# One gate pair fewer multiplied plainly: block products from pair 1, another order of the sums of h, other banks

## The reference, cut to what matters

```
h      = rms_norm(x, g) * (1 + scale) + shift
ga, gb = the last 2 x 1024 columns of h @ w_in
y_m    = (h_m * silu(za)) @ w_out_mlstm
y_a    = (o_a * silu(zb)) @ w_out_attn
merged = sigmoid(ga) * y_m + sigmoid(gb) * y_a
out    = rms_norm(x + gate * (merged @ w_out), g_final)
```

## Time and profile before

| what | us |
|---|---|
| median of 3 runs (lowest, highest) | 1432.43 (1432.05, 1433.26) |
| the profiled execution, its whole time | 1433.84 |
| its span, first to last instruction | 1432.0 |
| PE busy | 1409.8 (98%) |
| DVE, ACT, POOL busy | 816.3, 508.8, 382.7 |

### The profile page before, as it was taken

The page is one execution under the profiler, slowest core; times in us unless marked ns, Lnnn a source line. Parts: engine busy times, 40 slices in busy tenths (PEclk is TensorE's granted clock), DMA queues, the critical chain, the costliest instruction groups (busy, mean ns, idle before and its releaser), DMA issues.

```text
span 1432.0 us, 17208 instructions
## 1 busy us (share of the span) xinstructions
PE 1409.8 (98%) x6701; PEld 1178.1 (82%) x6701; DVE 816.3 (57%) x1367; ACT 508.8 (36%) x922; POOL 382.7 (27%) x209
## 2 busy tenths in 40 slices
PE   8999999999999999999999999999999999999996
PEld 6788888888888888888888888888888787888885
DVE  7876557366466745545474644457587526433565
ACT  7645223532323353232235323223443246111122
POOL 3032111222211122211111231111148873222541
PEclk9999999999999999999999999999999999999998
DMA  8321111142111114211111421111140306332443
GB/s 296 143 74 49 45 31 30 30 152 107 61 58 45 45 38 163 74 45 30 31 30 31 148 74 45 30 31 33 33 157 30 132 1 235 103 123 94 147 147 103
DMA packets 51818, 117.19 MB, mean 82 GB/s; under 512 B 20753, under 2 KB 20881, under 8 KB 51734
## 3 DMA queue, kind: packets, MB, share of 16 engines
q1 hardware_dynamic: 47786, 103.49, 22.6%
q10 hardware_dynamic: 2832, 8.53, 1.9%
q0 software_dynamic: 1120, 4.06, 1.0%
HBM read 100.64 MB, written 15.43 MB: 81 GB/s over the span
## 4 chain that ended last, share of the span: by engine, by line
PE 89%; DVE 4%; DMA 3%; ACT 2%; POOL 1%; issue 1%; SPq 0%; DVEq 0%; ACTq 0%; POOLq 0%
PE banks L532 25%; PE banks L534 25%; PE banks L533 25%; DMA x_rows<-in_x 2%; PE banks L825 2%; PE banks L815 2%; PE banks L776 2%; PE banks L782 2%; DVE y L2065 1%; PE banks L834 1%; PE banks L762 1%; PE banks L774 1%; PE banks L497 1%; PE banks L523 1%; PE banks L498 1%
## 5 line engine op out<-in xcount | busy, mean ns | idle before, releaser
L672 POOL TENSOR_TENSOR wlo<-wraw,whi 128x1024 fp32r<-128x1024 f32 x77 | 197.8, 2569 | 850.3 <-ACT whi L912 833.6
L532 PE MATMUL banks<-h_hi,whi 128*128 128x512 f32 x1000 | 400.3, 400 | 2.8 <-POOL wlo L1569 2.5
L534 PE MATMUL banks<-h_hi,wlo 128*128 128x512 f32 x1000 | 391.3, 391 | 0.0
L533 PE MATMUL banks<-h_lo,whi 128*128 128x512 f32 x1000 | 390.1, 390 | 0.0
L532 PEld LDWEIGHTS banks<-h_hi,whi 128*128 128x128 f32 x1000 | 188.4, 188 | 40.5 <-DVE sig_c L1843 2.2
L534 PEld LDWEIGHTS banks<-h_hi,wlo 128*128 128x128 f32 x1000 | 188.0, 188 | 40.2
L533 PEld LDWEIGHTS banks<-h_lo,whi 128*128 128x128 f32 x1000 | 188.6, 189 | 36.8
L912 ACT ACTIVATE whi<-wraw 128x1024 fp32r<-128x1024 f32 x75 | 78.9, 1053 | 83.8 <-PE banks L534 73.7
L534 PE MATMUL banks<-whi,h_lo 128*128 128x512 f32 x240 | 93.4, 389 | 0.0
L532 PE MATMUL banks<-whi,h_hi 128*128 128x512 f32 x240 | 93.4, 389 | 0.0
L533 PE MATMUL banks<-wlo,h_hi 128*128 128x512 f32 x240 | 93.4, 389 | 0.0
(11 more groups left out here) (377 smaller groups left out, 2592.2 us busy)
## 6 DMA issues: line engine op xcount, KB each, us to landing
wraw<-in_w_all SPq DMA_DIRECT2D x92, 512.0 KB, 3.7
s_wada<-in_w_ada_cols SPq DMA_DIRECT2D x16, 512.0 KB, 6.7
raw_lo<-in_x SPq DMA_DIRECT2D x8, 512.0 KB, 9.3
qm<-group_weights SPq DMA_DIRECT2D x8, 512.0 KB, 6.5
mlstm_branch<-xc SPq DMA_DIRECT2D x8, 512.0 KB, 9.4
part<-in_w_ada_gate SPq DMA_DIRECT2D x16, 256.0 KB, 3.6
sig_c<-in_w_all SPq DMA_DIRECT2D x8, 512.0 KB, 4.0
um_lo_raw<-mlstm_branch SPq DMA_DIRECT2D x8, 512.0 KB, 5.4
```

The source lines that it names most:

```text
L532: t_.matmul(out, w_hi, x_hi, start=first, stop=False)
L533: t_.matmul(out, w_hi, x_lo, start=False, stop=False)
L534: return t_.matmul(out, w_lo, x_hi, start=False, stop=last)
L672: nc.gpsimd.tensor_tensor(wlo[:, hi, :], wraw[:, q % 2, :], whi[:, hi, :].bitcast(F32), ALU.subtract).then_inc(w_split, 1)
```

## The change

1. `FIRST = 1`: only pair 0 is multiplied plainly; pairs 1 to 7 go through block products. Pair 1's weights stay where they were loaded (the ring), pair 2's now go to `sig` (`IN_SIG` gains 2), and `pair_high`, which made the high parts of pair 1's plain weights, goes.
2. DVE makes t3 third and t4 last; ACT's list has t3's halves among the first weights and t4's after the third and fourth products' turns; the products of the first block pair come in the order (1, 5, 6, 2, 7, 3, 4).
3. The plain pair's four half products go to banks 0, 4, 6, 7 instead of 1, 3, 0, 2, with their waits, and the block products start at bank 1.
4. In `project_tokens`, head 0, first chunk: tiles 0, 1, 4, 5 first and 2, 3, 6, 7 second.
5. `merge_groups` is cut into `join_two` (two scalings, one addition) and `join_third` (the rest). For the last head they stand in pair 2, the one between `upper_left` and `lower_half`, the other after `upper_right`; before, all six stood after pair 2's additions.

The diff, cut to its core:

```diff
@@ -713,9 +713,13 @@
...
                     pe.wait_ge(pv_kept, i * 12 + 1)
-                for c in range(4 * late, 4 * late + 4):
+                tiles = range(4 * late, 4 * late + 4) if i or n > VO else ((0, 1, 4, 5), (2, 3, 6, 7))[late]
+                for c in tiles:
                     if (i, n, c) == (0, VO, 2):
                         pe.wait_ge(gate_parts, 2)
+                    if (i, n, c) == (0, VO, 4):
+                        for h in range(2):
+                            pe.wait_ge(kept[h], XA + 2)
                     if (n, c) == (VO + (i == 0), NCH - 1):
@@ -1307,11 +1311,14 @@
...
-            def merge_groups(j):
+            def join_two(j):
...
                 step(v.tensor_tensor(order(num[0], 1), order(num[0], 1), stored(num[1], 1), ALU.add))
+            def join_third(j):
                 scale_group(j, 2)
@@ -1331,7 +1338,8 @@
...
                     if i:
-                        merge_groups(i - 1)
+                        join_two(i - 1)
+                        join_third(i - 1)
                 if i == 0 and n == 4:
@@ -1374,21 +1382,22 @@
...
             silu_zb()
-        T["shared"]["merge_groups"] = merge_groups
+        T["shared"]["join_two"], T["shared"]["join_third"] = join_two, join_third
...
 PRODUCTS = 7
-IN_SIG = (3, 5, 6, 7)
-FIRST = 2
+IN_SIG = (2, 3, 5, 6, 7)
+FIRST = 1
+PLAIN_BANKS = {(0, 1): 0, (1, 1): 4, (0, 0): 6, (1, 0): 7}
 TOTAL = PRODUCTS * (KT - FIRST)
...
-    return (1, 5, 6, 2, 4, 3, 7) if p == FIRST else (5, 4, 6, 7, 1, 2, 3) if p == KT - 1 else (5, 1, 2, 4, 6, 7, 3)
+    return (1, 5, 6, 2, 7, 3, 4) if p == FIRST else (5, 4, 6, 7, 1, 2, 3) if p == KT - 1 else (5, 1, 2, 4, 6, 7, 3)
@@ -1450,7 +1459,7 @@
...
     t_raw, t_hi_done, t_lo_done = T["t_raw"], sem("t_hi_done"), sem("t_lo_done")
-    turn_of = {1: 0, 2: 1, 4: 2, 3: 3}
+    turn_of = {1: 0, 2: 1, 3: 2, 4: 3}
     s_added, s_high, s_split, gprod = sem("s_added"), sem("s_high"), sem("s_split"), sem("gprod")
@@ -1467,7 +1476,7 @@
...
     whi4, wlo4 = (w[:].rearrange("p b (j c) -> p (b j) c", j=2) for w in (whi, wlo))
-    bank = lambda p, j: ps[:, at_product(p, j) % 8, :]
+    bank = lambda p, j: ps[:, (at_product(p, j) + 1) % 8, :]
     b_raw = [um_raw[:, k, :] if k < KT else ua_raw[:, k - KT, :] for k in range(KB)]
@@ -1475,7 +1484,7 @@
...
         def load_pair(p):
-            if p == 3:
+            if p in (2, 3):
                 sp.wait_ge(acc_out, 16)
@@ -1486,9 +1495,7 @@
...
                 sp.wait_ge(w_in[c], 16 * (Q0 // 2 + p))
-                if p == FIRST:
-                    sp.wait_ge(w_split, SPLIT0 + 2 * FIRST - 1 + c)
-                elif p not in IN_SIG:
+                if p not in IN_SIG:
                     before = max(e for e in range(p) if e not in IN_SIG)
@@ -1601,25 +1608,27 @@
...
             pe.wait_ge(w_split, SPLIT0 + 2 * p + j + 1)
-            if p:
+            if h == 0:
                 pe.wait_ge(masked, 24 * HEADS + 1)
...
                 pe.wait_ge(pv_kept, 12 * HEADS + 1)
-                pe.wait_ge(out_used, 4 * HEADS + 4)
             elif j == 0:
-                pe.wait_ge(kept[h], HEADS * MAIN + 1)
+                pe.wait_ge(kept[0], HEADS * MAIN + 1)
             else:
...
             for k in range(KT):
-                mm = three_pass(t_, ps[:, 4 * p + 2 * j + h, :], whi[:, j, k * P:(k + 1) * P], wlo[:, j, k * P:(k + 1) * P],
+                mm = three_pass(t_, ps[:, PLAIN_BANKS[j, h], :], whi[:, j, k * P:(k + 1) * P], wlo[:, j, k * P:(k + 1) * P],
                                 h_hi[:, k, tok], h_lo[:, k, tok], k == 0, k == KT - 1)
...
+            if o == 0:
+                pe.wait_ge(kept[1], HEADS * MAIN + 1)
             if o < 8:
-                pe.wait_ge(sig_done, 4 * (o // 4) + 4)
+                if o >= 3:
+                    pe.wait_ge(sig_done, 4)
             else:
@@ -1681,13 +1690,7 @@
...
             act.wait_ge(proj, PROJ0 + 4 * p + 1 + 2 * (1 - h) + j)
-            A(sig[p][:, j, h * HALF:(h + 1) * HALF], ps[:, 4 * p + 2 * j + h, :], ACT.Sigmoid).then_inc(sig_done, 1)
-        def pair_high(j):
-            act.wait_ge(proj, PROJ0 + 3 + j)
-            act.wait_ge(w_in[j], 16 * (Q0 // 2 + 2))
-            A(whi[:, j, :], raw[:, j, :], ACT.Copy).then_inc(w_high, 1)
+            A(sig[p][:, j, h * HALF:(h + 1) * HALF], ps[:, PLAIN_BANKS[j, h], :], ACT.Sigmoid).then_inc(sig_done, 1)
@@ -1759,21 +1762,14 @@
...
         sum_high(2, t2_hi, t2_raw)
-        pair_high(0)
-        first_sigmoid(0, 0, 0)
-        pair_high(1)
-        first_sigmoid(0, 1, 0)
-        first_sigmoid(1, 0, 1)
-        sum_high(4, t4_hi, t4_raw)
-        first_sigmoid(1, 1, 1)
         weight_high(FIRST, 1)
         weight_high(FIRST, 5)
-        first_sigmoid(1, 0, 0)
+        first_sigmoid(0, 0, 0)
         half_high(3, t3_hi, t3_raw, 0)
...
         weight_high(FIRST, 2)
+        first_sigmoid(0, 1, 0)
         half_high(3, t3_hi, t3_raw, 1)
-        first_sigmoid(1, 1, 0)
         order_ = [(p, j) for p in range(FIRST, KT) for j in products_of(p)]
@@ -1781,6 +1777,8 @@
...
                 weight_high(*order_[o + 4])
+            if o in (2, 3):
+                half_high(4, t4_hi, t4_raw, o - 2)
             if p > FIRST and j == products_of(p)[1]:
@@ -1891,21 +1889,23 @@
...
         sum_low(2, t2_hi, t2_lo, t2_raw)
+        dve.wait_ge(proj, PROJ0 + 4 * (FIRST - 1) + 2)
+        sum_raw(t3_raw, [(f(h_hi[:, KH:, RIGHT]), f(t3_lo), sub), (f(t3_hi), sub), (f(h_lo[:, KH:, RIGHT]), add)])
+        sum_low(3, t3_hi, t3_lo, t3_raw)
         for q in range(2):
...
         sum_low(4, t4_hi, t4_lo, t4_raw)
-        dve.wait_ge(proj, PROJ0 + 4 * (FIRST - 1) + 2)
-        sum_raw(t3_raw, [(f(h_hi[:, KH:, RIGHT]), f(t3_lo), sub), (f(t3_hi), sub), (f(h_lo[:, KH:, RIGHT]), add)])
-        sum_low(3, t3_hi, t3_lo, t3_raw)
         for p in range(FIRST, KT - 1):
...
             upper_left(p)
+            if p == 2:
+                T["shared"]["join_two"](HEADS - 1)
             lower_half(p)
             upper_right(p)
-            if p == FIRST:
-                T["shared"]["merge_groups"](HEADS - 1)
+            if p == 2:
+                T["shared"]["join_third"](HEADS - 1)
         for k in range(4):
```

## The result

The changed kernel takes 1451.56 us (1449.86 to 1451.95), the one before 1432.28: a ratio of 1.0131 with a 95% interval of [1.0119, 1.0143]. The forecast was 1442.6 with a range of 1434 to 1449. The sign was right and the place of most of the loss too; the size was not, and the time lies outside the range.

What follows compares the result with a forecast made beforehand. PE, busy 98% of the span, was taken as the bound; +14.9 us (parts 1, 3, 4 and the clock), -1.0 and -3.7 gave +10.2: 1444.0 against the profiled execution, 1442.6 by the median, range 1434 to 1449.

Steps and rivals of the forecast that it cites:

- Part 1: Pair 1 on PE goes from 96 to 84 matmuls: 2.7 us less.
- Part 2: First head's token tiles: reordering removes PE's wait for banks ACT has not emptied, 1.0 us less, bounds 0 and 1.05.
- Part 3: Start of merge stage: first plain product no longer waits for ACT's bank, 0.3 us less, counted as 0.
- Part 4: Pair 1: DVE's sums and POOL's operations take turns, t4 done at 1091.5, product 4 starts at 1091.6 instead of 1075.6.
- The clock: Pair 1, after the stall of 10 us before product 4: slow PE clock costs 2.1 us, bounds 0 and 4.
- Part 5: Last head's join cut in two: pair 4's stall and slow clock go, 3.7 us less; bounds 3.7 less, 3.7 more.
- gone or under 0.5 us: Sign to look for in the new trace: PE's POOL wait in pair 4 gone or under 0.5 us.
- My third rival: The join's stall stays, in pair 3 or 4: +13.9, 1446.3 us; chance 15%.
- Pairs 4 to 7 and everything behind them keep their distances: From pair 4 to the kernel's end the timing between stages stays as before; no term in the sum.
- The first rival: Pair 1's sums on DVE and POOL's work run side by side, all gains count: 7.7 us less, 1424.7; chance 8%.

Runs made afterwards that it cites:

- The experiments on both engines: Changed kernel with pair 1's four POOL combinations left out, 1447.13 us; changed kernel with t4's raw sum on DVE cut to one operation a half, 1441.27 us.
- the left-out combinations: The changed kernel with pair 1's four combinations of weights on POOL left out, plain quarters used instead: 1447.13 us, ratio 1.0101.

## Why the prediction was wrong in size

Step by step, against the profiled executions (predicted +10.2, measured +18.1). The 7.9 us between them are 4.0 in pair 7, 2.4 in the join's pairs, 1.3 of late setup, 0.9 at the end of pair 1, less 0.8 behind pair 7 (7.8 as rounded). The first two are steps of the prediction that were wrong:

- **Part 1** (2.7 us of matmuls less): they are gone from the list, but part 4 swallows the gain, as forecast.
- **Part 2, the tiles** (-1.0): right, and tried alone. It doesn't show in the trace's totals, since that execution's setup was 1.3 us late. (These two nearly cancel, which is why the times that the forecast gave without the tiles can be held against the trace as they are below; that is luck.)
- **Part 3, the banks** (counted as 0): the merge stage starts 0.6 us sooner for it, and part 4 takes it back. Right.
- **Part 4, the sums and the low parts:** the mechanism, the turns of 1.15 and 1.1 us, the wait of product 1 (predicted 1.4, measured 1.5 by the starts), of product 6 ("some 4 us", 3.7), of product 4 (some 10, 9.8) and the end of t4 (1091.5, measured 1092.4) are close to what was predicted. The experiments on both engines bear it out. Pair 1 ended at 1097.6, forecast 1096.4 (1095.4 with the tiles taken off, and 1096.7 with the late setup added).
- **The clock** (2.1 us behind the long wait): product 4 took 5.0 us instead of 2.7, so 2.3. Right. That it would also be slow behind product 6's wait was not said; the long wait swallowed that.
- **Part 5, the join** (-3.7): mis-sized, by 2.4 us in these traces. I gave the low part of pair 3's second product 0.4 us of slack; it came 0.6 us late, and pair 4's came 1.4 us late, where "gone or under 0.5 us" was the sign to look for. I counted fewer stretched operations in pair 4's own chain, and not that the chain starts 2.0 us later because the join now stretches the low parts of pair 3 ahead of it. My third rival, that the stall stays, with 15%, was nearer. And 1.7 of the 3.7 us was a slow clock that other executions with the same stall don't have. The forecast by the median also took off the 1.4 us by which the profiled execution lies above it, and 1433.84 less those 1.7 us is 1432.2, the median itself: so this clock was very likely subtracted twice, and 1442.6 was too low by 1.4 us even by its own terms.
- **"Pairs 4 to 7 and everything behind them keep their distances":** this step failed, for 4.0 us in the traces, and it is the one that puts the time outside the range. I had listed everything that is timed by a pair's own order and missed what is timed by a count over all pairs. The edit of FIRST changes TOTAL, and with it the phase of the ring against pair 7's end. It could be read in the code. With the ring's phase put right the changed kernel takes 1446.69 us, inside the range.
- **The first rival**, that DVE and POOL run side by side: refuted by the left-out combinations, 4.3 us for four POOL operations. The Trainium skill, SBUF — State Buffer, section "Who interferes with whom", says that a DVE instruction with two inputs in SBUF contends with a GpSimd instruction that reads SBUF; the trace agrees.

What stays open: the 0.8 us by which the part behind pair 7 is shorter, whether the 0.9 us between the forecast and the measured end of t4 is the one POOL operation more (its price of 1.1 us would cover it), and the late setup of some executions. None was tried alone.

## What to carry to other kernels

Fewer matmuls help only as long as the engines that prepare them fit under what is left: where two of them take turns, as DVE and POOL do here, price the preparation as the sum of both lists, not engine by engine. When a loop's bounds change, look for every modulo and every "last use" that is computed over the whole count; its phase is an edit too. A stall that comes from a saturated pair of engines was moved here by reordering, not removed: four kernels with the join placed otherwise took 1431.35 to 1432.11 us, against 1431.15 with the join left where it was.

## What the runs showed of the hardware

In the merge stage of the twelve traces the clock's answer to a gap was not the same for like gaps. Behind gaps of 1.1 to 1.9 us in PE's starts (sixteen, 1.87 the longest) it stayed full. Behind those of 2.0 to 3.7 us it fell, 2.00, 1.99 and 2.49 among them, with one exception: of the five gaps of 3.35 or 3.36 us at the same place in pair 7, four were followed by a mean clock of 0.66 to 0.69 over five us and one by 1.00. Behind 8.6 to 11.1 us it was low every time (0.53 to 0.60). Where it was low, PE took steps of 0.43 us instead of 0.227, mostly from the first matmul on, and lost some 1.6 to 3.0 us: as much as 2.8 and 3.0 behind two of the gaps of 3.7 us, and 1.6 behind the two others. A profile taken in one execution can thus carry a term that the median hasn't.
